# One block of transposes a round later in an attention, two orders changed at the border of two norms, and a quarter of the result scaled by ScalarE

## The reference

```python
def rmsnorm(x, g):
    xf = x.astype(jnp.float32)
    y = xf * lax.rsqrt(jnp.mean(xf * xf, axis=-1, keepdims=True) + NORM_EPS)
    return (y * g.astype(jnp.float32)).astype(x.dtype)

# first_block, layer 1: 16 query heads, 4 key heads, 64 wide, 256 tokens
x = x + gqa_axial_mixer(rmsnorm(x, mix_norm_c[i]), gqa_w_q[i], gqa_w_kv[i], ...)
x = x + swiglu(rmsnorm(x, ffn_norm[layer]), ffn_w_in[layer], ffn_w_out[layer])
...
return rmsnorm(x, final_norm)                     # the end of first_block
# second_block, layer 0 begins on that result with a norm of its own
x = x + FFN_RES_WEIGHT * swiglu_ffn(rms_norm(x, ffn1_norm[l]), ffn1_w1[l], ffn1_w2[l])
...
return rms_norm(x, final_norm)                    # the end of second_block, the result
```

## Time and profile before

| | us |
|---|---|
| median of three runs | 1881.63 (1881.41 to 1882.01) |
| the profiled execution | 1882.02 |
| its span, first to last instruction | 1880.2 |
| TensorE busy | 1863.6 |
| VectorE busy | 1340.4 |
| ScalarE busy | 861.0 |
| GpSimd busy | 124.3 |

### The profile page before, as it was taken

How to read it: one execution, slowest core, us unless ns; L and a number is a source line. 1 busy time by engine, 2 the same in 40 slices (tenths; PEclk the granted TensorE clock), 3 DMA queues, 4 the chain that set the end, 5 groups by cost and what they waited for, 6 DMA issues and landing times.

```text
span 1880.2 us, 28201 instructions
## 1 busy us (share of the span) xinstructions
PE 1863.6 (99%) x10664; PEld 1601.1 (85%) x10664; DVE 1340.4 (71%) x1697; ACT 861.0 (46%) x1107; POOL 124.3 (7%) x155
## 2 busy tenths in 40 slices
PE   9999999999999999999999999999999999999998
PEld 8998888888888888888977888888888897788887
DVE  5676767776767776776876677677777767677777
ACT  5554434474334444344375433443335337644333
POOL 1001200230000100000300100010000020000000
PEclk9999999999999999999999999999999999999999
DMA  7423555425555565544434465556554444455453
GB/s 307 180 90 148 199 181 187 171 82 203 212 191 188 224 223 200 181 167 169 178 137 162 175 227 184 201 218 229 197 182 175 164 166 168 147 189 213 180 199 113
DMA packets 48548, 343.46 MB, mean 183 GB/s; under 512 B 5472, under 2 KB 5504, under 8 KB 8784
## 3 DMA queue, kind: packets, MB, share of 16 engines
q1 hardware_dynamic: 43200, 310.92, 45.5%
q0 software_dynamic: 5264, 31.35, 4.4%
HBM read 341.20 MB, written 1.05 MB: 182 GB/s over the span
## 4 chain that ended last, share of the span: by engine, by line
PE 66%; issue 0%; DVE 0%; POOL 0%; ACT 0%; DVEq 0%; POOLq 0%
PE bank L1068 16%; PE bank L856 12%; PE bank L858 12%; PE bank L857 12%; PE bank L1067 7%; PE bank L919 2%; PE bank L1070 1%; PE bank L1147 1%; PE bank L1519 1%; PE bank L964 1%; PE bank L959 1%; PE bank L960 1%; PE bank L1443 0%; PE bank L1381 0%; PE bank L1508 0%
## 5 line engine op out<-in xcount | busy, mean ns | idle before, releaser
L2065 DVE TENSOR_TENSOR wlo<-raw,whi 128x2048 fp32r<-128x2048 f32 x292 | 672.1, 2304 | 223.2 <-ACT whi L1586 222.7
L1586 ACT ACTIVATE whi<-raw 128x2048 fp32r<-128x2048 f32 x293 | 559.3, 1910 | 256.4 <-PE bank L858 252.3
L1068 PE MATMUL bank<-ysp,whi 128*128 128x512 f32 x1920 | 666.1, 396 | 0.0
L1067 PE MATMUL bank<-ysp,wlo 128*128 128x256 f32 x1680 | 468.6, 279 | 0.0
L1068 PEld LDWEIGHTS bank<-ysp,whi 128*128 128x128 f32 x1920 | 347.7, 188 | 67.0
L1067 PEld LDWEIGHTS bank<-ysp,wlo 128*128 128x128 f32 x1680 | 316.8, 189 | 10.7
L1669 ACT ACTIVATE sg<-sg 128x256 f32<-128x256 f32 x120 | 50.2, 418 | 468.2 <-DVE sg L2262 468.2
L856 PE MATMUL bank<-whi,ysp 128*128 128x512 f32 (+3 forms) x592 | 217.3, 367 | 0.3 <-DVE wlo L2065 0.3
L858 PE MATMUL bank<-whi,ysp 128*128 128x512 f32 (+3 forms) x592 | 212.8, 359 | 0.0
L857 PE MATMUL bank<-wlo,ysp 128*128 128x512 f32 (+3 forms) x592 | 212.4, 359 | 0.0
L856 PE MATMUL bank<-whi,hl 128*128 128x512 f32 x528 | 206.0, 390 | 0.0
(11 more groups left out here) (359 smaller groups left out, 2356.7 us busy)
## 6 DMA issues: line engine op xcount, KB each, us to landing
raw<-stream SPq DMA_DIRECT2D x294, 1024.0 KB, 4.8
sr<-side POOLq DMA_DIRECT2D x10, 1024.0 KB, 5.2
gbc<-gains POOLq DMA_DIRECT2D x11, 512.0 KB, 3.9
cw<-small POOLq DMA_DIRECT2D x2, 2048.0 KB, 10.7
gbias<-gate_rows POOLq DMA_DIRECT2D x6, 512.0 KB, 4.3
dbias<-dilb POOLq DMA_DIRECT2D x1, 2304.0 KB, 12.8
lng<-rows POOLq DMA_DIRECT2D x2, 1024.0 KB, 5.2
tab<-second POOLq DMA_DIRECT2D x1, 1724.0 KB, 15.0
```

The lines of the kernel that those rows point to most:

```text
L1067: pe.matmul(o[:, 0, :], lo[:, k, cols], yh[:, k, :], start=False, stop=False, skip_group_check=True)
L1068: last = pe.matmul(o, hi[:, k, cols], ysp[:, :, k, :], start=k == 0, stop=k == 7)
L1586: act.activation(whi[s], raw[s], ACT.Copy).then_inc(hi_made, 1)
L2065: dve.tensor_tensor(wlo[s], raw[s], whi[s].bitcast(F32), ALU.subtract).then_inc(lo_made, 1)
```

## The change

Three edits. First, heads3 is turned in round 3 instead of round 2, and ScalarE's copy of it moves from the end of round 2 to the end of round 3, behind the tile split that already stands there. Second, at the border of the two norms (only for f = 2), TensorE makes both transposes of y's second token half after the eight matmuls of `first_half`'s second group, and VectorE makes the last quarter of z ahead of the low half of a transposed quarter. Third, in the last norm VectorE multiplies the last quarter of x by the gain into z, and ScalarE scales it into y while VectorE makes the quarter before it; SP waits for each with a semaphore of its own.

```diff
-        late_heads = {1: 2, 2: 3, 4: 4}
+        late_heads = {1: 2, 3: 3, 4: 4}
...
-            for q in range(2):
-                sp.wait_ge(y_ready, 47 + q)
+            for q, made in enumerate((last_dve, last_act)):
+                sp.wait_ge(made, 1)
                 sp.dma_start(out[:, 1, 512 * q:512 * q + 512], y[:, 1, 512 * q:512 * q + 512]).then_inc(out_done, 16)
...
+                def both_turns():
+                    turn(B, stage, n, 1, 0)
+                    turn(B, stage, n, 1, 1)
...
+                if twice:
+                    return {**late, (0, 8): both_turns}
+                return {**late, (0, 6): lambda: turn(B, stage, n, 1, 0), (0, 7): lambda: turn(B, stage, n, 1, 1)}
...
+                    if q and (0, 8) in late:
+                        late[(0, 8)]()
                     late[(0, 4 * q)]("D")
...
                 if i == 3:
                     ahead(B, "gqkv", 4)
-                if i == 2:
                     act.wait_ge(late_done, late_no("heads3") + 1)
                     act.activation(gqT[:, 4:6, :], bank2(0), ACT.Copy).then_inc(late_act, 1)
...
                     sumsq(8 + 3 * l)
+                    act.wait_ge(last_gained, 1)
+                    act.wait_ge(rstd_ready, POWERS_DOUBLE + POWERS * LAYERS)
+                    act.activation(y[:, 1, 512:D], z[:, 1, 512:D], ACT.Copy, scale=rstd[:, 1:2]).then_inc(last_act, 1)
...
                 add(3)
+                if not norm_stage:
+                    dve.wait_ge(x_ready, 4 * n)
+                    dve.tensor_tensor(z[:, 1, 512:D], x[:, 1, 512:D], gbc[:, 512:D], ALU.mult).then_inc(last_gained, 1)
                 half_mean(n, 1)
...
+                if not norm_stage:
+                    dve.wait_ge(rstd_ready, powers[0])
+                    dve.scalar_tensor_tensor(out=dst[:, 1, 0:512], in0=x[:, 1, 0:512], scalar=rstd[:, 1:2], in1=gbc[:, 0:512],
+                                             op0=ALU.mult, op1=ALU.mult).then_inc(last_dve, 1)
+                    return
...
                 add(3)
+                scaled(3)
                 lo_norm(then, norm_stage, 0, 1)
-                scaled(3)
                 means(1)
```

More of the change, by code:

```diff
@@ L589, in build @@
         out_done = sem("out_done")
+        last_gained = sem("last_gained")
+        last_dve = sem("last_dve")
+        last_act = sem("last_act")
         dve_link = [sem("dve_link0"), sem("dve_link1")]
@@ L934, in turn, with norm_late @@
                 batch(B, tb, [y[:, m, (4 * q + k) * P:(4 * q + k + 1) * P] for k in range(4)], bank=bank)
-            def norm_late(B, stage, n):
+            def norm_late(B, stage, n, twice=False):
+                def both_turns():
+                    turn(B, stage, n, 1, 0)
+                    turn(B, stage, n, 1, 1)
                 tb = B.plan.tb[stage]
-                return {(0, 0): lambda who: copied_by(B, tb + 1, who), (0, 4): lambda who: copied_by(B, tb + 2, who),
-                        (0, 6): lambda: turn(B, stage, n, 1, 0), (0, 7): lambda: turn(B, stage, n, 1, 1),
+                late = {(0, 0): lambda who: copied_by(B, tb + 1, who), (0, 4): lambda who: copied_by(B, tb + 2, who),
                         (1, 0): lambda: copied(B, tb + 3), (1, 4): lambda: copied(B, tb + 4)}
+                if twice:
+                    return {**late, (0, 8): both_turns}
+                return {**late, (0, 6): lambda: turn(B, stage, n, 1, 0), (0, 7): lambda: turn(B, stage, n, 1, 1)}
             def first_half(B, stage, tile, late):
@@ L1100, in pair @@
                     down(B, chunks, i - 1, 3 * i)
-                token_pair(B, stage, 0, t0, True, norm_late(B, norm_stage, n))
+                token_pair(B, stage, 0, t0, True, norm_late(B, norm_stage, n, f == 2))
                 hidden_turn(0)
@@ L2173, in ending @@
                 add(3)
+                if not norm_stage:
+                    dve.wait_ge(x_ready, 4 * n)
+                    dve.tensor_tensor(z[:, 1, 512:D], x[:, 1, 512:D], gbc[:, 512:D], ALU.mult).then_inc(last_gained, 1)
                 half_mean(n, 1)
-                if norm_stage:
-                    lo_norm(then or B, norm_stage, 0, 1)
+                if not norm_stage:
[3 more added lines that the diff above has]
+                    return
+                lo_norm(then or B, norm_stage, 0, 1)
                 dve.wait_ge(rstd_ready, powers[0])
```

## The result

| | before | after |
|---|---|---|
| median, us | 1881.63 (1881.27 to 1882.08, 7 runs) | 1887.65 (1886.75 to 1889.54, 7 runs) |
| the profiled execution, us | 1882.02 | 1887.53 |
| its span, us | 1880.2 | 1885.7 |
| TensorE busy, us | 1863.6 | 1866.4 |

The changed kernel is slower: after over before is 1.0032, with a 95% interval of 1.0022 to 1.0042. That is 6.0 us by the medians, where 4.3 were forecast, and 0.65 us above the top of the range. The runs also lie wider apart than before: 2.8 us instead of 0.8.

What follows compares the result with a forecast made beforehand. TensorE, busy in 99% of the span, was taken as the bound; wait 3.84 plus clock 1.4 less border 0.95 plus ending 0 gave +4.3 us on 1882.02 us, about 1885.9 us by the median; range 1883.8 to 1887.0.

Steps and rivals of the forecast that it cites:

- The wait: Attention, round 4: scores wait for ScalarE's heads3 copy behind the split, start at 402.59; costs 3.84 us of TensorE.
- the sum: Whole kernel: 3.84 + 1.4 - 0.95 + 0 = +4.3 us, about 1885.9 us by the median.
- The clock: Attention, round 4: TensorE's clock falls in the gap of 3.7 us and costs 1.4 us more.
- The upper bound of 2.2 us: High end of the clock's price, from the opening: 36 passes in 6.23 us where 4.0 us would do.
- Rival (d): Low clock as long as at the opening or longer, 2.2 us or more; border gain 0.7: 1887 us and above; chance 0.06.
- Round 2: Attention: TensorE's transposes of probabilities can't start before 391.76, against 391.82; gain 0, with 0.06 us as other end.
- Rival (b): Attention, round 3: nmx gets ahead of POOL's add, 0.6 less, gap 3.1 us: 1883.9 to 1885.3 us; chance 0.15.
- Part 2: Border of the two norms: the idle of 0.99 us goes; gains 0.95 us, or 0.7 if y is no earlier.
- Part 3: Ending: second DMA issued some 0.3 us earlier, but transfers are the limit; gives 0, ends -0.3 and +0.1.

Runs made afterwards that it cites:

- e5: The changed kernel with unread filler matmuls in both TensorE idles, 7 in round 2 and 14 in round 4; 1884.87 us, ratio 1.0018.
- e2: The kernel before with the second and third edits but not the heads3 edit; 1881.21 us, ratio 0.9996.
- e1: The kernel before with the heads3 edit alone (turned in round 3, copied behind the split); 1888.43 us, ratio 1.0034.
- e3: The changed kernel with 14 unread filler matmuls in the gap of round 4 only; 1887.6 us, ratio 1.0027.
- e4: The changed kernel with ScalarE's heads3 copy ahead of the split in round 3, not behind it; 1884.61 us, ratio 1.0011.
- e7: The changed kernel with 7 unread filler matmuls in the idle of round 2 only; 1887.49 us, ratio 1.0031.
- e6: The changed kernel with the heads3 copy ahead of the split and 7 filler matmuls in the idle of round 2; 1884.6 us, ratio 1.0015.
- e12: The kernel before with heads3's transposes still in round 2, but behind the probabilities' transposes and the outputs; 1882.35 us, ratio 1.0009.
- e9: The kernel before with only the second edit, the order at the border of the two norms; 1881.15 us, ratio 0.9996.
- e10: The kernel before with only the third edit, the last quarter of the result scaled by ScalarE; 1881.87 us, ratio 0.9999.
- e11: The kernel before with the second and third edits, the ending's second output DMA writing 256 of its 512 columns; 1880.67 us.

## Why the prediction was wrong

**The wait: right.** Scores(4) were put at 402.59 in the times of the trace before; they came at 402.37 in an execution that stands 0.24 us earlier (the scores of round 2 at 388.84, in the trace before at 389.08), so at 402.61. By e5, where the clock stays up, the scores of round 5 are at 406.76 in a trace that stands 0.12 us earlier than before (388.96 to 389.08), so at 406.88 against 403.08: 3.80 us for the 3.84 of the sum. By the medians e5 less e2 is 3.7 us, or 4.2 us with each set against its own runs of before.

**The clock: the step that failed.** It fell, as forecast, but cost 6.95 - 4.26 = 2.7 us and not 1.4; it is the only term of the sum that is off by more than 0.25 us, and it alone carries the time past 1887.0. Two things were wrong in how it was priced. The upper bound of 2.2 us came from the opening, the only place where matmuls ran slowly for some time; it is no bound: the passes there were slow for some 4 us, while behind a gap the low stretch was 6.8 us long in this trace and in those of e1, e3, e4 and e7. And the value was taken below that bound since "part of the low stretch can lie in the gap itself". In the changed kernel 1.2 us of it do (401.2 to 402.37), but the low stretch is 6.8 us long, and 5.6 us of it lie on work. Half of that time is lost, 2.8 us, as the measured 2.7 show. In e6, 3.4 us on work cost 1.6. The Trainium skill (TensorE: Matmul & The Clock Gate, "Terms") puts the penalty at the time at the reduced rate times the share of the clock that is missing, which at half rate is half of it. These two traces agree with it if only the low time on work is counted; e4's doesn't, as 6.8 us on work cost 1.5 us there, since a later wait took up the rest. Rival (d), a low clock at the price of the opening or more, is what happened to the clock, though part 2 didn't shrink as (d) had it; (d) had 0.06.

That a fall would come was forecast from a single one, 2.1 us after the last matmul of the kernel before. The fall came (the lowest runs of the changed kernel and of e7 are 1886.75 and 1886.39, the highest of e5 is 1885.05), but 2.1 us is no measure of the gap that it takes: over the profiles of all fourteen kernels the clock falls between 2.1 us (before) and 5.3 us (e12) after the last matmul, though that matmul ends the same stretch of work in all of them.

**Round 2: right in time, wrong in what it sets off.** The transposes start at 391.74, which is 391.98 in the times of the trace before, 0.16 us later than there (391.82) and not ahead of it, as worked out. But heads3 had cut the idle: it stood for 1.07 us and then worked. Without it TensorE stands 1.75 us in one stretch, and I had written that idles up to 1.5 us show no fall and looked no further, though the edit itself made this one longer. In the changed kernel's profile the clock didn't fall there; in e3's and e4's it did. What a fall there costs the changed kernel no profile shows. In e3, with the fillers, it cost as much as the later one does (its middle group 1887.49 to 1887.83, e7's runs mostly 1887.40 to 1887.85). It explains why filling only the gap didn't help in seven of e3's runs, and perhaps the run at 1889.54, the only one of the changed kernel with a mean clock of 0.996; the median needs nothing but the later fall, which its profile shows and to which e7's runs come without the idle of round 2.

**Rival (b): did not happen.** nmx of round 3 came at 396.99 and took 0.60 us, and POOL's add had again started ahead of it:

```profile
396.99 0.60 DVE L2364 TENSOR_SCALAR nmx<-mx 128x4 f32<-128x4 f32 x1
```

```profile
396.83 0.73 POOL L784 TENSOR_TENSOR gr<-gtp 128x256 f32<-128x256 f32 x1
```

It ended at 397.59, 0.03 us after the add. Here luck helped the sum: the scores of round 3 came 0.15 us later than in the trace before (394.46 + 0.24 against 394.55), which the sum had at 0, but nmx ended with the add in both, at 397.83 and 397.81.

**Part 2: right.** From the scores of round 5 to the second token half it is 643.01 - 409.32 = 233.69 us, before 637.66 - 403.08 = 234.58: 0.89 us for the 0.95 of the sum. The last quarter of z one place earlier let VectorE's y start without the wait for ScalarE's square, and all of the idle of 0.99 us is gone. The medians of e9 give 0.74 us.

**Part 3: right.** 0.02 us less by e10, and the reason given, that the transfers are the limit, is borne out by e11.

**The sum again.** 3.80 + 2.69 - 0.89 + 0 = 5.60 us by the traces, and the profiled executions are 5.51 us apart. The medians are 6.02 us apart, since the profiled execution of before stood 0.39 us above its median and that of after 0.12 us under. Had the clock been priced so, the forecast would have been 1887.2 us.

**The version to keep** is part 2 alone, or parts 2 and 3: 0.75 us under the kernel before, with all eleven runs of e2 under the lowest of the 28 runs beside them (1881.31 against 1881.68). Its interval, 0.9987 to 1.0005, still holds 1. Fillers can't save part 1: with them it costs its 3.8 us. With the copy ahead of the split (e4, e6) the fastest runs stand at 1883 us, still above the kernel before; a version of it with both idles filled was not run.

## What to carry to other kernels

When an edit makes the busiest engine wait, price two things: the wait, and half of the time that a low clock would lie on the work behind it, less what a later wait of the same engine takes up (e4: 1.5 us left of 3.4); for the second take the length of a low stretch from a trace that has a whole one, and don't bound it by another phase of the kernel. Work that stands inside an idle is worth something even where it isn't on the critical path: moving it out can join two short idles into one that brings the clock down. And where a loss can have two causes, take both away at once before judging either, and look at the single runs: by the medians each of two fillers alone showed hardly a gain, both together 2.8 us. See in the trace, too, whether a filler still stands in a wait: in e3's profile the fillers ran 1.0 us past it.

## What the runs showed of the hardware

- TensorE's clock fell in some runs behind idles of 1.75 us (e3), 1.91 us (e4) and 1.77 us (e6), each shorter than the 2.1 us at the end of the kernel before. TensorE was already at work again when the clock fell, for 1.3 us in e3, 1.8 us in e4 and 0.3 us in e6. In other runs of the same kernels it didn't fall, by their times and mean clocks (0.999 against 0.996 to 0.998). The runs of one kernel then stand in groups with 1.3 to 2.3 us between them (e3, e4), and here a wide spread was itself a sign of it: e5, with both idles filled, spreads 0.43 us, e3 4.7 us.
- Behind the gaps of 3.57 to 3.58 us (the changed kernel, e1, e7) the profiles show the clock falling 2.0 to 2.4 us into the gap, and no run of the changed kernel or of e7 (lowest 1886.39) comes near those of e5 (1884.62 to 1885.05).
- After the last matmul the clock fell 2.1 us (before) to 5.3 us (e12) later, by the windows of fourteen profiles.
- The fillers, 7 and 14 matmuls of 128x128 (1.83 and 3.34 us), kept the clock at 1.00 from 386 to 412 us in e5.
- A low stretch was 6.8 us long in the profiles of the changed kernel (401.2 to 408.0) and of e3 (393.0 to 399.8), with TensorE busy all the time in the latter, and 3.4 us in e6 (401.0 to 404.4).
- At the opening the record of the clock reads 1.00 all the time, though matmuls take some 0.2 us each in the first 4 us, about twice what they take later. This is the profile of the kernel before, windows as in the earlier trace rows:

```profile
1.00:4.40 3.40, 3.40 (x16) 3.40 (x17) 0.00 (x0) 1.03 (x1) 0.84 (x2) 1.00 0.65 159
```

So there the durations have to be read, not the clock's column.
